# A duo's transposes in the beat of its products, and three attentions of the first block as one chain

## The chip, the cores and the metric

The kernel runs on one core of one Trainium2 chip, in one launch. The metric is device time in microseconds (us) of that core; lower is better. PE is TensorE, DVE is VectorE, ACT is ScalarE, POOL is GpSimd and SP is SyncE, which issues the loads of the weights.

## The reference

One transformer block with three attentions, followed by two layers of a second block, all on `x` of 512 tokens by 1024 channels in fp32. Cut to what matters here:

```python
# first block: three attentions on one normed h, then a gated merge, then an MLP
oa = diff_attention(aq, ak, av, lam, bias_a)                  # "att_a": 4 heads, two softmax maps each, w = p0 - lam*p1
oa = rms_norm(oa, diff_subln) * (1.0 - lam_init)
ob = banded_attention(bq, bk, bv, bias_b, B_WINDOW, sinks)    # "att_b": 8 heads, window of 128, a sink in the softmax
oc = g0 * o_cmp + g1 * o_sel + g2 * o_win                     # "att_c": compressed, selected and window branch
x = x + sum_n(sigmoid(mg_n) * (branch_n @ w_branch_n)) @ w_out
x = x + square(relu(rms_norm(x) @ w_up)) @ w_down
# second block, twice: SwiGLU, mixer, SwiGLU
ya = chunked_relpos_attention(qa, ka, va, ...)                # "att_a2"
yc = forgetting_attention(qc, kc, vc, ...)                    # "att_c2"
# each attention: s = q k^T * scale + bias; p = softmax(mask(s)); o = p v
# (queries and keys are rms-normed per head: a "root" each in the kernel)
```

## The kernel before

Everything is held transposed, channels in the 128 partitions and tokens along the free axis. A dense product of the weights is a *group*: 8 chunks of 128 input channels, each chunk three matmuls (L1202 to L1204: high by high, high by low and low by high parts of an fp32 split), 128x512 or, for tokens in partitions, 128 tokens by 408 or 512. POOL splits each weight piece into its two parts. PSUM has 8 banks; a group takes one of its ring.

An attention is cut into *duos*: two heads (or two maps) of one block of 128 queries. There are 16 in att_a, att_b, att_a2 and att_c2, and 48 in att_c, where each block has three branches. A duo goes through these steps:

- `score` (PE, L1275): two products of queries and keys, into banks 0 and 1; then `minima` on DVE (L1704) adds the bias, writes the duo's tile of `s_sb` (two duos fit) and leaves `row_min`.
- `exp` (ACT, L1445, twice), then the inverses of the sums (DVE, L1717, in att_c L1721 and L1730, in a column of the sum bank 4).
- `prob` (ACT, L1463; in att_a L1455, L1457 and then DVE L1734, which joins the two maps): the scaled probabilities.
- `turn` (PE, L1292): one transpose of 128x128 for each block of keys, into bank 2 (att_a, att_b) or banks 2 and 3. It waits for `probs`.
- `copy` (ACT, L1478): the transposes to `pt_sb`, of which there is one. It waits for the turn and for the products of the duo before.
- `pv` (PE, L1312 in att_a, L1317 elsewhere): the products with the values, into bank 5. Behind the last duo of a pair the result leaves the bank, and in att_a it goes through a root of its own ("differential": ACT L1405 and L1407, PE L1261, ACT L1415, DVE L1663 and L1673, ACT L1545, DVE L1676).

The banks of the scores come free for the next duo when att_a's `probs` are there (the second map lies in bank 1 until then), elsewhere when `row_min` is.

The order on every engine is written out by a planner that runs in Python before the build: `plan` puts steps into one list, `ORDER`, and every engine walks this list and emits its part of each step. Nothing is reordered later. `attend` gives the duos of one attention as *beats*, each a function with a weight; `weave` runs a beat and then as many *stretches* (two chunks of a group, so six matmuls) as the beat's share of the weight asks for. Beat j holds the scores of duo j + 2, the turn of duo j + 1 and the products of duo j. Within the beat of att_a, of att_b and att_c and att_c2, and of att_a2 the order of these differs (the three branches at the end of `attend`).

A root of queries or keys is spread over the stretches by `LATER`: its sum on PE two stretches after the group, the two halves of its reciprocal (DVE L1663) three and four after. `ROOTED` is the last root whose steps stand in `ORDER`. `HELD` says for each bank what its next user must wait for. Each `weave` ends with `flush`, which puts out all of `LATER`.

The load of the bias of the pair after next (`load_bias`) stands right behind the last scores of a pair. ACT issues it, after a wait for that duo's `row_min` (L1491).

## Time and profile before

| | us |
|---|---|
| median of 3 runs (lowest, highest) | 3510.7 (3504.93, 3511.44) |
| the profiled execution's own time | 3509.4 |
| its span | 3507.6 |
| PE busy | 3407.7 (97%) |
| POOL busy | 2370.5 (68%) |
| DVE busy | 1186.1 (34%) |
| ACT busy | 883.3 (25%) |

By the times of their scores (L1275) the stages lie at: att_a 98 to 233, att_b 233 to 332, att_c 332 to 545, att_a2 1460 to 1590 and 2706 to 2836, att_c2 behind each of these. What lies between is dense products.

The profile is of one execution. An engine's row in a timeline has its start, its duration, and in brackets how long the engine was idle before it and which instruction released it. A wait can be small in the sum and still decide, since PE is busy nearly all the time: what PE is idle is what could be gained, with what its clock loses behind a wait.

### The profile page before, as it was taken

Reading aid. Unit: us, or ns where it says so; the run is one execution under the profiler, and the core shown is the slowest. Engines: PE = TensorE matmul, PEld = TensorE weight load, DVE = VectorE, ACT = ScalarE, POOL = GpSimd, SP = SyncE. Lnnn points to the kernel's source line nnn. Section 1 sums busy time; section 2 is a strip of 40 time slices with the busy share of each in tenths; the row PEclk is TensorE's granted clock in tenths of the full one; section 3 lists DMA queues with packets and bytes.
Section 4 is the critical chain, followed back from the end, with each engine's and each line's share of the span. In section 5 each row is a group of like instructions: output and inputs, shape, how many; then the busy total and the mean of one; then the engine's idle time right before and its main releaser. Section 6 shows DMA issues by size and latency. Waiting matters only on the chain.

```text
span 3507.6 us, 42466 instructions
## 1 busy us (share of the span) xinstructions
PE 3407.7 (97%) x17034; PEld 2738.9 (78%) x17034; DVE 1186.1 (34%) x2514; ACT 883.3 (25%) x1876; POOL 2370.5 (68%) x1242
## 2 busy tenths in 40 slices
PE   8978999999999999999999999999999999999999
PEld 6655777988898888667779888888887677798887
DVE  6554342433443234552223111332245422241111
ACT  2656552211120002354312000210012543221000
POOL 7514547787778776645677877687775546678775
PEclk9999999999999999999999999999999999999999
DMA  3212223344535442212232222254432222223232
GB/s 142 68 60 82 73 64 102 143 175 168 187 132 198 175 165 94 73 58 82 85 103 102 96 97 95 80 218 167 170 129 73 67 75 79 82 97 103 98 100 73
DMA packets 104771, 388.08 MB, mean 111 GB/s; under 512 B 12016, under 2 KB 12400, under 8 KB 98432
## 3 DMA queue, kind: packets, MB, share of 16 engines
q1 hardware_dynamic: 88272, 292.76, 25.3%
q10 hardware_dynamic: 16304, 92.62, 6.9%
q8 instruction: 135, 2.21, 0.3%
q14 instruction: 60, 0.49, 0.0%
HBM read 383.20 MB, written 2.13 MB: 110 GB/s over the span
## 4 chain that ended last, share of the span: by engine, by line
PE 91%; DVE 4%; ACT 4%; issue 1%; ACTq 0%; DVEq 0%
PE psum L1202 28%; PE psum L1204 27%; PE psum L1203 27%; PE psum L1275 2%; PE psum L1317 2%; PE psum L1292 2%; PE psum L1261 1%; DVE rs_t L1663 1%; DVE s_sb L1704 1%; ACT s_sb L1445 0%; ACT s_sb L1463 0%; ACT L1445 0%; ACT L1415 0%; PE psum L1253 0%; ACT rs_t L1415 0%
## 5 line engine op out<-in xcount | busy, mean ns | idle before, releaser
L1170 POOL TENSOR_TENSOR w_hi<-raw,ones 128x1024 fp32r<-128x1024 f32 (+2 forms) x593 | 1041.3, 1756 | 981.0 <-PE psum L1204 973.1
L1173 POOL TENSOR_TENSOR w_lo<-raw,w_hi 128x1024 fp32r<-128x1024 f32 (+2 forms) x593 | 1316.4, 2220 | 46.5
L1202 PE MATMUL psum<-h_hi,w_hi 128*128 128x512 f32 (+2 forms) x2912 | 1141.9, 392 | 30.5 <-DVE r L1679 20.5
L1204 PE MATMUL psum<-h_hi,w_lo 128*128 128x512 f32 (+2 forms) x2912 | 1106.2, 380 | 0.0
L1203 PE MATMUL psum<-h_lo,w_hi 128*128 128x512 f32 (+2 forms) x2912 | 1105.6, 380 | 0.0
L1202 PEld LDWEIGHTS psum<-h_hi,w_hi 128*128 128x128 f32 (+1 forms) x2912 | 550.3, 189 | 167.4 <-issue 33.9
L1204 PEld LDWEIGHTS psum<-h_hi,w_lo 128*128 128x128 f32 (+1 forms) x2912 | 550.1, 189 | 106.7
L1203 PEld LDWEIGHTS psum<-h_lo,w_hi 128*128 128x128 f32 (+1 forms) x2912 | 551.0, 189 | 101.0 <-issue 7.2
L1202 PE MATMUL psum<-a_hi,w_hi 128*128 128x512 f32 (+1 forms) x1064 | 392.5, 369 | 0.0
L1203 PE MATMUL psum<-a_lo,w_hi 128*128 128x512 f32 (+1 forms) x1064 | 391.9, 368 | 0.0
L1204 PE MATMUL psum<-a_hi,w_lo 128*128 128x512 f32 (+1 forms) x1064 | 391.8, 368 | 0.0
L1930 DVE TENSOR_TENSOR psum<-g_sb,psum 128x512 f32<-128x512 f32 x120 | 83.5, 696 | 734.3 <-PE psum L1204 641.4
L1595 ACT ACTIVATE g_sb<-psum 128x512 f32<-128x512 f32 x120 | 71.8, 598 | 919.5 <-PE psum L1204 832.9
L1204 PEld LDWEIGHTS psum<-a_hi,w_lo 128*128 128x128 f32 x1064 | 200.6, 188 | 33.5
L1203 PEld LDWEIGHTS psum<-a_lo,w_hi 128*128 128x128 f32 x1064 | 200.6, 189 | 33.4
L1202 PEld LDWEIGHTS psum<-a_hi,w_hi 128*128 128x128 f32 x1064 | 200.6, 189 | 33.3
L1939 DVE SCALAR_TENSOR_TENSOR x<-psum,res,x 128x512 f32<-128x512 f32 (+1 forms) x132 | 88.4, 669 | 357.5 <-PE psum L1204 357.5
L1602 ACT ACTIVATE a_hi<-psum 128x512 fp32r<-128x512 f32 x120 | 71.8, 598 | 493.9 <-DVE psum L1930 493.9
L1704 DVE CUSTOM_DVE_ANT_0 s_sb<-psum,bias_t 128x128 f32<-128x128 f32 (+3 forms) x224 | 100.8, 487 | 233.1 <-PE psum L1275 159.9
L1445 ACT ACTIVATE s_sb<-s_sb,row_min 128x128 f32<-128x128 f32 (+6 forms) x272 | 140.1, 517 | 130.5 <-DVE row_min L1704 127.3
L1795 DVE CUSTOM_DVE_ANT_0 ada_t<-ada_t,psum 128x1024 f32<-128x1024 f32 x144 | 167.7, 1215 | 0.0
L1663 DVE RECIPROCAL rs_t<-rs_t 128x256 f32<-128x256 f32 x78 | 132.3, 1729 | 68.2 <-ACT rs_t L1415 68.2
(198 smaller groups left out, 3305.0 us busy)
## 6 DMA issues: line engine op xcount, KB each, us to landing
raw<-weights_dram SPq DMA_DIRECT2D x487, 512.0 KB, 3.4
ada_t<-ada_dram ACTq DMA_DIRECT2D x48, 1536.0 KB, 7.1
raw<-weights_dram SPq DMA_DIRECT2D x76, 256.0 KB, 2.7
raw<-weights_dram SPq DMA_DIRECT2D x32, 384.0 KB, 3.1
bias_t<-biases_dram ACTq DMA_DIRECT2D x36, 256.0 KB, 2.9
bias_t<-cum_dram ACTq DMA_DIRECT2D x16, 256.0 KB, 4.1
out_dram<-x SPq DMA_DIRECT2D x8, 256.0 KB, 2.0
raw<-weights_dram SPq DMA_DIRECT2D x4, 408.0 KB, 3.2
```

Source lines behind the costliest of these rows:

```text
L1170: nc.gpsimd.tensor_tensor(high, piece, ones[:, 0:1].to_broadcast([P, n]), ALU.mult)\
L1173: nc.gpsimd.tensor_tensor(w_lo[:, p % NR, 0:n], piece, high.bitcast(F32), ALU.subtract)\
L1202: mm(dst, lh, rh, start=first, stop=False)
L1203: mm(dst, lh, rl, start=False, stop=False)
L1204: return mm(dst, ll, rh, start=False, stop=last)
L1445: ins = fn(to, s, ACT.Exp, scale=-1.0, bias=row_min[:, r:r + 1], accum_out=row_sum[:, r:r + 1])
L1595: fn(g_sb[:, g.index % 2, :], bank(g.bank), ACT.Silu if gated else ACT.Relu)\
L1663: v.reciprocal(r, r).then_inc(sem["qk_inverse"], 1)
L1704: ins = v.tensor_tensor_reduce(out=s[:, 0:w], in0=bank(SCORE_BANKS[half], w), in1=tile, scale=-1.0, scalar=sinks[:, half:half + 1] if o el ...
L1795: ins = v.tensor_tensor_reduce(out=part, in0=part, in1=c_bcast, scale=1.0, scalar=0.0, op0=ALU.mult, op1=ALU.add, accum_out=mod_raw[:, l, ...
L1930: v.tensor_tensor(bank(g.bank), g_sb[:, n % 2, :], bank(g.bank), ALU.mult)\
L1939: v.scalar_tensor_tensor(x[:, d, cs], bank(g.bank)[:, cs], res_of(which, d), x[:, d, cs], ALU.mult, ALU.add).then_inc(sem["x_added"], 1)
```

## The change

- In all attentions the turn and the copy of a duo move from the beat before its products into the beat of its products: beat j now holds the scores of duo j + 2, the turn of duo j, its copy and its products.
- All attentions have one order: turn, scores, copy; exps; products; low part and `prob`. The branches for att_a and for att_a2 are gone.
- A `Chain` holds the duos of one or of several attentions. The first block's three are one chain: the last two beats of att_a hold the first two scores of att_b, and those of att_b the first two of att_c. `flush` stands only behind the chain's last attention.
- Where a step needs a root whose steps still stand in `LATER`, the planner pulls them forward: before scores whose queries or keys are not rooted, before a turn whose bank a root still holds, and before scores of the compressed branch.
- The wait for the sum bank in att_c is taken at `prob` and not at the scores, and `HELD` names the inverses as its last user.

```diff
--- before.py
+++ after.py
@@ -190,9 +190,10 @@
         pass
 
 
-def weave(kind, layer, jobs):
-
-    beats = attend(kind, layer)
+def weave(chain, kind, jobs):
+
+
+    beats = attend(chain, kind)
     total, weight = sum(job.n for job in jobs if isinstance(job, Group)), sum(w for _, w in beats)
     q, done, passed_by = stretches(jobs), 0, 0
     for beat, w in beats:
@@ -202,7 +203,8 @@
             done += next(q, total)
     for _ in q:
         pass
-    flush()
+    if chain.duos[-1].kind == kind:
+        flush()
 
 
 
@@ -504,16 +506,29 @@
     return (Q_AT[u.kind], 4 + u.pair)
 
 
-def attend(kind, layer):
-
-
-    duos = duos_of(kind, layer)
+@dataclass(eq=False)
+class Chain:
+
+    duos: list
+    masks: list
+
+
+def chain_of(kinds, layer):
+    return Chain([u for kind in kinds for u in duos_of(kind, layer)], [])
+
+
+def attend(chain, kind):
+
+
+    duos, masks = chain.duos, chain.masks
     n = len(duos)
-    masks = []
+    own = [j for j in range(n) if duos[j].kind == kind]
+    lo, hi = (own[0] if own[0] else -2), own[-1] + 1
 
     def scores(j):
         if j + 2 < n:
             u = duos[j + 2]
+            kind = u.kind
             u.n = tick("scores")
             for name in ("probs", "transposed", "pt_copied", "pv"):
                 assert tick(name) == u.n
@@ -522,17 +537,19 @@
             u.s_before = [take(b) for b in SCORE_BANKS]
             HELD[SCORE_BANKS[0]] = HELD[SCORE_BANKS[1]] = ("probs", u.n) if kind == "att_a" else ("row_min", 2 * u.n)
             u.need = max(READY[(Q_AT[kind], u.pair)], READY[keys_of(u)])
-            if kind == "att_c":
-                u.inv_before = take(SUM_BANK)
+            while u.need > ROOTED[0] or u.br == "cmp" and "kc_done" not in TOTAL:
+                LATER.pop(0)[1]()
             put("score", u)
             if u.last:
                 load_bias(u.bias.n + 2, 2 * u.n)
                 masks.append([2, u.bias.n + 2])
 
     def turns(j):
-        if 0 <= j + 1 < n:
-            u = duos[j + 1]
-            u.t_before = [take(b) for b in (T_BANKS[:1] if kind in ("att_a", "att_b") else T_BANKS)]
+        if 0 <= j < n:
+            u = duos[j]
+            u.t_before = [take(b) for b in (T_BANKS[:1] if u.kind in ("att_a", "att_b") else T_BANKS)]
+            while any(at and at[0] == "qk_out" and at[1] > ROOTED[0] for at in u.t_before):
+                LATER.pop(0)[1]()
             for b in T_BANKS[:len(u.t_before)]:
                 HELD[b] = ("pt_copied", u.n)
             put("turn", u)
@@ -540,6 +557,7 @@
     def products(j):
         if 0 <= j:
             u = duos[j]
+            kind = u.kind
             if u.first:
                 u.o_before = take(O_BANK)
             u.need_v = READY[V_AT[kind]]
@@ -561,34 +579,32 @@
                 mask_bias(e[1])
 
     def copy(j):
-        if 0 <= j + 1 < n:
-            put("copy", duos[j + 1])
+        if 0 <= j < n:
+            put("copy", duos[j])
 
     def exps(j):
         if j + 2 < n:
             put("exp", duos[j + 2])
 
     def low(j):
-        if 0 <= j and duos[j].last and kind != "att_a":
+        if 0 <= j and duos[j].last and duos[j].kind != "att_a":
             put("blow", duos[j])
 
     def scale(j):
         if j + 2 < n:
-            put("prob", duos[j + 2])
+            u = duos[j + 2]
+            if u.kind == "att_c":
+                u.inv_before = take(SUM_BANK)
+                HELD[SUM_BANK] = ("inverses", 2 * u.n)
+            put("prob", u)
 
     out = []
-    for j in range(-2, n):
+    for j in range(lo, hi):
         w = 1 + max([d.blocks for d in duos[max(0, j):j + 3]])
-        if kind == "att_a":
-            out += [(lambda j=j: scores(j), w), (lambda j=j: (exps(j), turns(j)), w),
-                    (lambda j=j: (products(j), copy(j), scale(j)), 2 * w)]
-        elif kind in ("att_b", "att_c", "att_c2"):
-            out += [(lambda j=j: (scores(j), products(j)), w), (lambda j=j: (exps(j), low(j)), w),
-                    (lambda j=j: (turns(j), copy(j)), w), (lambda j=j: scale(j), w)]
-        else:
-            out += [(lambda j=j: scores(j), w), (lambda j=j: (exps(j), turns(j)), w),
-                    (lambda j=j: (products(j), copy(j)), w), (lambda j=j: (low(j), scale(j)), w)]
-    return out + [(lambda: [mask_bias(b) for _, b in masks], 0)]
+
+        out += [(lambda j=j: (turns(j), scores(j), copy(j)), w), (lambda j=j: exps(j), w),
+                (lambda j=j: products(j), w), (lambda j=j: (low(j), scale(j)), w)]
+    return out + [(lambda: [mask_bias(b) for _, b in masks], 0)] * (hi == n)
 
 
 
@@ -864,9 +880,9 @@
             chain += shifts + [product]
     jobs += chain
     put("tables")
-    weave("att_a2", l, jobs)
+    weave(chain_of(("att_a2",), l), "att_a2", jobs)
     ring = MIX_RINGS["att_c2"]
-    weave("att_c2", l, merge((l + 1, 1), "br_b", "set", ring) + merge((l + 1, 0), "br_a", "mid", ring))
+    weave(chain_of(("att_c2",), l), "att_c2", merge((l + 1, 1), "br_b", "set", ring) + merge((l + 1, 0), "br_a", "mid", ring))
     if l == 0:
         tick("cond_loaded", 16)
         put("condload")
@@ -919,15 +935,16 @@
           normed(("ck", 4), "key", ("small", "gain", 7), ("k5", 2), ring),
           plain(("ck", 0), ("k5", 3), ring), plain(("ck", 1), ("k5", 4), ring)]
     tick("gate_tanh")
-    weave("att_a", 0, [ks[0]] + b + ks[1:] + token_groups(("vbc",), V_BC, "v_bc", ring)
+    chain = chain_of(("att_a", "att_b", "att_c"), 0)
+    weave(chain, "att_a", [ks[0]] + b + ks[1:] + token_groups(("vbc",), V_BC, "v_bc", ring)
           + [lambda: put("gates", TOTAL["plain_out"])])
 
     ring = MIX_RINGS["att_b"]
     cq = [normed(("cq", i), "query", ("small", "gain", 4), ("r2", i), ring) for i in range(4)]
     gather, hidden = compress(ring)
-    weave("att_b", 0, [lambda: gather(0), cq[0], lambda: gather(1), cq[1], hidden, cq[2], cq[3]])
+    weave(chain, "att_b", [lambda: gather(0), cq[0], lambda: gather(1), cq[1], hidden, cq[2], cq[3]])
     ring = MIX_RINGS["att_c"]
-    weave("att_c", 0, merge((0, 0), "br_a", "set", ring) + merge((0, 1), "br_b", "mid", ring))
+    weave(chain, "att_c", merge((0, 0), "br_a", "set", ring) + merge((0, 1), "br_b", "mid", ring))
     tick("cond_loaded", 16)
     put("condload")
     run_all(merge((0, 2), "br_c", "last"))
```

What this moves, at three places. In the functions of the engines the lines of the kernel after are 17 higher.

ScalarE in att_a, where the root of the second pair's result ends: `br_a` is that root's high part (it waits for `qk_out`, a result of DVE), the two rows with `row_sum` are a duo's exps, `pt_sb<-psum` is a copy. Before:

```order
L1491 DMA bias_t<-biases_dram 128x512 [waits row_min]
L1491 DMA bias_t<-biases_dram 128x512
L1545 ACTIVATE br_a<-psum 128x512 [waits qk_out]
L1445 ACT_TABLE_LOAD
L1445 ACTIVATE s_sb,row_sum<-s_sb,row_min 128x384
L1445 ACTIVATE psum,row_sum<-s_sb,row_min 128x384
L1478 ACTIVATE pt_sb<-psum 128x256 [waits pv,transposed]
L1455 ACTIVATE s_sb<-s_sb,row_inv 128x384 [waits inverses]
```

After:

```order
L1495 ACTIVATE pt_sb<-psum 128x512 [waits pv,transposed]
L1462 ACT_TABLE_LOAD
L1462 ACTIVATE s_sb,row_sum<-s_sb,row_min 128x384
L1462 ACTIVATE psum,row_sum<-s_sb,row_min 128x384
L1562 ACTIVATE br_a<-psum 128x512 [waits qk_out]
L1472 ACTIVATE s_sb<-s_sb,row_inv 128x384 [waits inverses]
L1474 ACTIVATE row_scale<-row_inv,neg_lam 128x1 [waits inverses]
```

The exps now stand ahead of `br_a`, and the copy stands ahead of the exps and no longer between them and `prob` (`s_sb<-s_sb,row_inv`); the bias's DMAs stand ahead of the copy.

ScalarE some duos later, at the last bias load of att_a. Before:

```order
L1545 ACTIVATE br_a<-psum 128x512 [waits qk_out]
L1491 DMA bias_t<-biases_dram 128x512 [waits row_min]
L1491 DMA bias_t<-biases_dram 128x512
L1445 ACTIVATE s_sb,row_sum<-s_sb,row_min 128x128
L1445 ACTIVATE psum,row_sum<-s_sb,row_min 128x128
L1478 ACTIVATE pt_sb<-psum 128x512 [waits pv,transposed]
```

After:

```order
L1562 ACTIVATE br_a<-psum 128x512 [waits qk_out]
L1508 DMA bias_t<-biases_dram 128x512 [waits row_min]
L1508 DMA bias_t<-biases_dram 128x512
L1495 ACTIVATE pt_sb<-psum 128x256 [waits pv,transposed]
L1462 ACTIVATE s_sb,row_sum<-s_sb,row_min 128x128
L1462 ACTIVATE psum,row_sum<-s_sb,row_min 128x128
```

The copy of the duo two before (128x256), which stood well ahead of these rows, now stands behind the two DMAs, and so behind the wait for `row_min`.

TensorE where att_b ends and att_c begins: `h_hi`, `w_hi` rows are dense products, `pt_sb,v_bc` the products with the values, `sq_t,cst` the sum of the last query root, `k_56,r_52` scores of att_c, `cst,s_sb` transposes. Before:

```order
L1203 MATMUL psum<-h_lo,w_hi 128x512
L1204 MATMUL psum<-h_hi,w_lo 128x512
L1317 MATMUL psum<-pt_sb,v_bc 64x128 [waits pt_copied]
L1317 MATMUL psum<-pt_sb,v_bc 64x128
L1261 MATMUL psum<-sq_t,cst 128x512 [waits qk_rooted,qk_squared]
L1275 MATMUL psum<-k_56,r_52 128x128 [waits row_min]
L1275 MATMUL psum<-k_56,r_52 128x128
L1202 MATMUL psum<-h_hi,w_hi 128x512 [waits w_lo,qk_out]
L1203 MATMUL psum<-h_lo,w_hi 128x512
```

After:

```order
L1220 MATMUL psum<-h_lo,w_hi 128x512
L1221 MATMUL psum<-h_hi,w_lo 128x512
L1334 MATMUL psum<-pt_sb,v_bc 64x128 [waits pt_copied]
L1334 MATMUL psum<-pt_sb,v_bc 64x128
L1278 MATMUL psum<-sq_t,cst 128x512 [waits inverses,qk_squared]
L1309 MATMUL psum<-cst,s_sb 128x128 [waits qk_out,probs]
L1309 MATMUL psum<-cst,s_sb 128x128
L1292 MATMUL psum<-kc_sb,r_52 128x31 [waits kc_done,row_min]
L1292 MATMUL psum<-kc_sb,r_52 128x31
L1219 MATMUL psum<-h_hi,w_hi 128x512 [waits w_lo]
```

Before, scores and two stretches of dense products stood behind the root's sum. Now a turn stands right behind it, and waits for that root (`qk_out`), since its second bank was the root's.

## Rows read from the trace of the kernel before

**Rows 1.** The page's busy times over the whole span, by engine.
```profile
...
PE 3407.7 (97%) x17034; PEld 2738.9 (78%) x17034; DVE 1186.1 (34%) x2514; ACT 883.3 (25%) x1876; POOL 2370.5 (68%) x1242
```

**Rows 2.** Windows, by stage: length, busy by engine, granted clock, DMA share, GB/s.
```profile
...
98.00:233.00 135.00, 114.19 (x522) 83.80 (x520) 69.68 (x146) 82.53 (x170) 54.09 (x35) 0.94 0.21 67
233.00:332.00 99.00, 74.87 (x450) 48.09 (x448) 57.56 (x169) 66.57 (x158) 33.49 (x28) 0.91 0.25 80
332.00:545.00 213.00, 212.33 (x1294) 151.43 (x1294) 77.01 (x389) 118.33 (x334) 102.90 (x67) 0.99 0.21 64
1460.00:1590.00 130.00, 122.12 (x615) 81.54 (x614) 59.14 (x152) 69.96 (x151) 62.79 (x32) 0.97 0.19 63
```

**Rows 3.** Waits of PE in att_a: us in total, times, longest.
```profile
...
PE psum L1275 <- DVE s_sb L1734: 15.0, 10, 5.6
PE psum L1261 <- DVE br_a L1676: 3.7, 1, 3.7
```

**Rows 4.** Waits of PE in att_b and at its two ends.
```profile
...
PE psum L1275 <- DVE row_min L1704: 9.2, 3, 5.9
PE psum L1317 <- ACT pt_sb L1478: 8.9, 6, 1.9
PE psum L1362 <- ACT cmp_g L1566: 3.0, 1, 3.0
```

**Rows 5.** Timeline around att_a's longest wait: start, us, engine, instruction, [idle before].
```profile
...
191.35 0.60 ACT L1545 ACTIVATE br_a<-psum 128x512 fp32r<-128x512 f32 x1 [5.18 <-DVE psum L1673]
...
191.98 0.69 DVE L1676 TENSOR_TENSOR br_a<-psum,br_a 128x512 fp32r<-128x512 f32 x1 [0.66 <-ACT br_a L1545]
...
193.26 0.61 ACT L1445 ACTIVATE s_sb<-s_sb,row_min 128x384 f32<-128x384 f32 x1
...
196.23 1.65 PE L1275 MATMUL psum<-r 64*128 64x384 f32 x4 [5.57 <-DVE s_sb L1734]
```

**Rows 6.** Timeline in att_a: a copy behind the products, and the next scores.
```profile
...
203.06 0.49 ACT L1478 ACTIVATE pt_sb<-psum 128x384 f32<-128x384 f32 x1 [3.09 <-PE psum L1312]
...
204.95 0.70 PE L1275 MATMUL psum<-r 64*128 64x256 f32 x4 [0.87 <-DVE s_sb L1734]
```

**Rows 7.** Timeline where att_a ends and att_b begins.
```profile
...
235.07 3.36 DVE L1663 RECIPROCAL rs_t<-rs_t 128x256 f32<-128x256 f32 x2 [1.86 <-ACT rs_t L1415]
...
241.38 1.22 PE L1275 MATMUL psum<-k,r 64*128 64x256 f32 x4 [5.88 <-DVE row_min L1704]
```

**Rows 8.** Timeline where att_b ends and att_c begins.
```profile
...
320.52 1.12 PE L1261 MATMUL psum<-sq_t,cst 128*128 128x512 f32 x2 [0.32 <-ACT sq_t L1405]
...
323.00 3.36 DVE L1663 RECIPROCAL rs_t<-rs_t 128x256 f32<-128x256 f32 x2 [1.31 <-ACT rs_t L1415]
...
327.62 0.49 PE L1275 MATMUL psum<-k,r 64*128 64x128 f32 x4 [2.60 <-DVE row_min L1704]
```

**Rows 9.** Timeline, bias loads: the wait for one, the issues of another.
```profile
...
118.50 1.28 ACT L1415 ACT_TABLE_LOAD   x1 [2.66 <-DVE row_min L1704]
...
188.89 0.82 ACTq L1491 DMA_DIRECT2D bias_t<-biases_dram  x2
```

**Rows 10.** Groups by form (copies), and of the page (reciprocals of the roots).
```profile
...
L1478 ACT ACTIVATE pt_sb<-psum 128x512 f32<-128x512 f32 x40 | 23.5, 588 | 29.0 <-PE psum L1292 24.1 <-PE psum L1312 3.6 <-PE psum L1317 1.1
...
L1663 DVE RECIPROCAL rs_t<-rs_t 128x256 f32<-128x256 f32 x78 | 132.3, 1729 | 68.2 <-ACT rs_t L1415 68.2
```

**Rows 11.** Timeline of PE: the products that follow a group of transposes.
```profile
...
111.32 0.48 PE L1202 MATMUL psum<-h_hi,w_hi 128*128 128x512 f32 x1
111.64 0.40 PE L1203 MATMUL psum<-h_lo,w_hi 128*128 128x512 f32 x1
111.87 0.40 PE L1204 MATMUL psum<-h_hi,w_lo 128*128 128x512 f32 x1
```

**Rows 12.** Windows right behind the two longest waits.
```profile
...
194.00:200.00 6.00, 3.77 (x10) 2.54 (x11) 2.16 (x8) 3.31 (x10) 3.26 (x5) 0.59 0.01 5
242.00:248.00 6.00, 4.92 (x15) 3.10 (x12) 4.96 (x17) 2.27 (x9) 0.00 (x0) 0.50 0.00 0
```

## The prediction

> **What bounds the kernel now.** I read the page first. PE is busy 3407.7 of 3507.6 us [rows 1], so all that any reordering can win is PE's idle 100 us, and what its clock loses. The change moves no work on or off PE. So the next view is the windows by stage [rows 2]: att_a has 135.00 - 114.19 = 20.8 us of idle PE and a mean granted clock of 0.94, att_b 24.1 us and 0.91, att_c 0.7 us, att_a2 7.9 us. A clock of 0.94 means that (1 - 0.94) x 2 x 135 = 16 us lay at the lower of the two levels, 0.91 in att_b another 18 us; half of such time is lost where PE has work, at its busy share of 80% some 14 us in all. The stages that the change touches hold 45 us of waits and 14 us of clock in att_a and att_b, and little elsewhere. Then the waits of these two stages: in att_a PE waits for att_a's joined maps before it may overwrite their banks, 15.0 us in ten waits, and once 3.7 us for the sum bank [rows 3]; in att_b it waits for `row_min` 9.2 us, for copies 8.9 us and for the compressed branch's gelu 3.0 us [rows 4]. Last the timeline at the longest of them, for what stands ahead of what on ACT and DVE.
>
> **att_a, joined maps: 6 us less.** A duo's scores need the probabilities of the duo before, so scores, minima, exps, inverses, `prob` and the joining are a loop. In the longest wait (5.57 us) the exps stood behind the root's `br_a` on ACT, which started at 191.35, and a table load, and began at 193.26 [rows 5]. In the new order they stand ahead of it. What is late next is DVE: its inverses come behind L1676, which ends at 191.98 + 0.69 = 192.67. From the first exp to the scores it took 196.23 - 193.26 = 2.97 us, less two exps of 0.6 some 1.75 us: scores at 194.4 in place of 196.2, so 1.8 us less. A copy no longer stands between exps and `prob`; in [rows 6] it waited for the products until 203.06 and the scores then waited 0.87 us: such a wait goes. The other nine waits sum to 15.0 - 5.6 = 9.4 us; where a reciprocal of a root is what is late (half of them) the copy's move does nothing. I take 9.4 to 5. The 3.7 us for the sum bank falls to about 2.3, because the joining and two inverses now stand behind the root's last steps and not between them. The remaining 2.1 us (20.8 - 15.0 - 3.7) go with the early turn. Against that stand: `prob` now comes one sub-beat later, so in five duos a half reciprocal and the scaling of a root (1.73 + 0.75 us, the latter an estimate by rows of 128x512 like L1676's 0.69) slip between exps and inverses. Part of it lies beside the exps; I take 2 us. And the bias loads, below, 1.5 us. Sum: -1.8 - 4.4 - 1.4 - 2.1 + 2 + 1.5 = -6. Bounds: all 20.8 gone, or 16 us of root work fully exposed, +12.
>
> **From att_a to att_b: 5.5 us less.** Before, the last result's root ran with nothing behind it: its reciprocals took 3.36 us of DVE from 235.07, the first minima of att_b came behind them, and PE waited 5.88 us [rows 7]. Now two scores of att_b stand ahead of that root and its sum stands between att_b's first groups. What is late next is the gather of the compressed branch and the same reciprocals on DVE, ahead of `row_min` of the fourth duo; by their lengths I leave 1.5 us, and a turn's wait of 1 us behind it goes too: -5.5. Bounds -7 and 0.
>
> **att_b's middle: 0.** From turn to products lies one stretch in 13 of 16 duos and none in three; before it was one in 12 and none in four. So no cover is lost. ACT has half a beat more before a copy is due, which would take perhaps 4 of the 8.9 us [rows 4]. The bias loads take it back: a load waits for the minima of the duo just scored, and the copy is now queued behind it. ACT sat idle 2.66 us for this once, and two issues take 0.82 us [rows 9]; with a copy of 0.59 us [rows 10] that is about 2.5 us behind the scores, against one stretch of six products at 0.23 us [rows 11], 1.4 us. So 1.1 us at each of four pairs: +4.4. Bounds -8 and +10.
>
> **From att_b to att_c: 3.5 us more.** The last query root ends in bank 3, which the first turn of att_c needs. Before, scores and two stretches stood behind that root's sum at 320.52, and the wait was 2.60 us at 327.62 and about 1 more behind it, 4 with the small one ahead [rows 8]. Now the turn stands right behind the sum, and queued behind that turn is all of PE. The sum itself waits for the inverses of the second duo. From the end of the group: a square, two exps, the high part and `prob`, 2.8 us of ACT, a table load of 1.28, the square root 0.7, reciprocals 3.36 [rows 8], the scaling 0.75: 8.9 us, of which PE works 1.5. That is 7.4 for 4. Bounds 0 and +7.
>
> **att_c, att_a2, att_c2: 4 us more.** In att_c ten duos have no stretch between turn and products (before two), mostly short ones whose copy the scores cover; of four bias loads two have none and two have one: 2 x 2 + 2 x 1.1 minus what their waits hid, 4 us; bounds 0 and +12. In att_a2 two stretches (before five) stay between turn and products, 2.7 us for a copy and the rest of ACT's queue; a few waits for `prob` go, a few for copies come: 0, bounds -5 and +8. att_c2 keeps its three: 0.
>
> **Fewer switches on PE: 3.4 us less.** Between dense products and small ones PE changes 34 times less (43 to 33 groups in att_a, 48 to 36 in each att_a2, four more in att_b and att_c; counted in the order). The first product behind a group of transposes starts its successor 0.32 us later, the next ones 0.23 [rows 11]: 0.1 us each. By the Trainium skill, TensorE: Matmul & The Clock Gate, in "Part 2: What happens when you issue a matmul", the loads of weights are pulled ahead of products in flight, which would make such a switch free, and the sum 3.4 us less good. The row has 0.1 us, so the trace does not agree.
>
> **Clock: 5 us less.** The longest waits are followed by windows with a granted clock of 0.59 and 0.50 [rows 12]. One of the two (att_b's start) should go and one stay, and the new wait at att_c keeps its own. Of 14 us I take 5 back. Bounds +5 and -14.
>
> **Sum.** -6 - 5.5 + 0 + 3.5 + 4 - 3.4 - 5 = -12.4. The profiled execution took 3509.4 us, 1.8 more than its span, so 3497.0. The median of the runs is 1.3 above that execution: 3498.
>
> **Rivals.** (1) *It loosens nearly all.* With prompt copies the loop in att_a falls under its beat, att_b runs without waits but for gelu, and the clock stays up: 30 of 45 us, 9 of clock and the switches: 3468. For it: the mean beat in att_a is 7.5 us, a loop without roots some 5. Against it: roots, table loads and reciprocals stay where they are. (2) *Given back.* The waits for joined maps turn into waits for copies, which now have 1 or 2 stretches of cover instead of 3 or 4 in att_a: gains and losses meet within 0.2%, about 3508. For it: ACT is busy 82.53 of 135 us there, and a copy stands behind whatever ACT has late. (3) *Slower: `prob` behind the root in att_a.* The bank is held until the maps are joined. If the 16 us of reciprocals, scalings and square roots that now stand between exps and `prob` in five duos lie fully open, the clock falls behind each, and I get 3509.4 + 12 - 5.5 + 3.5 + 4 - 3.4 + 5 = 3525. It decides when PE's waits for the joined maps pass 25 us. Against it: the same reciprocals stood ahead of the next minima in the same loop before. (4) *It doesn't do what it says:* a forced root stands somewhere else too. The order shows it at att_c's start alone.
>
> **How the numbers follow.** My case 0.45, (1) 0.15, (2) 0.22, (3) 0.14, (4) 0.04. About 0.2% (7 us) is what a measurement here tells from no change, so faster means under 3503.7. My case is faster for three quarters of its width, and with (1) and some of (2) that gives 0.56 faster, 0.26 within, 0.18 slower. The range of 8 in 10 goes from 3474 to 3518.
>
> **What would show it.** Right: PE's waits for att_a's maps at 8 to 11 us, the wait at att_b's start under 3 us, att_b's window some 5 us shorter, a wait of 6 to 8 us for a query root at the first transposes of att_c, copies waited for behind bias loads, a clock of 0.96 in att_a. Wrong: longer waits for the maps, copies waited for by PE in att_a or att_a2 for more than 8 us, or att_c longer by more than 6.

## The result, and the profile after

The changed kernel takes 3547.8 us (median of 4 runs, 3546.7 to 3549.0) against 3511.1 for the kernel before (4 runs). The ratio is 1.0109, 95% interval 1.0093 to 1.0125: slower by 37 us. The forecast was 3498, 12 us faster. The profiled execution has a span of 3545.0 us, 37.4 longer than before.

The page's busy times answer to [rows 1]:

```profile
...
PE 3423.5 (97%) x17034; PEld 2745.5 (77%) x17034; DVE 1192.2 (34%) x2514; ACT 887.7 (25%) x1876; POOL 2369.9 (67%) x1242
```

PE is busy 15.8 us more for the same 17034 instructions, and idle 121.5 us, 21.6 more. By stage, windows of the changed kernel (length, busy by engine, granted clock, DMA share, GB/s), which answer to [rows 2]:

```profile
...
96.00:221.00 125.00, 104.05 (x479) 75.73 (x477) 69.24 (x145) 80.06 (x162) 52.76 (x35) 0.96 0.17 58
221.00:327.00 106.00, 77.45 (x474) 50.67 (x473) 59.95 (x169) 68.44 (x163) 33.80 (x29) 0.93 0.27 90
327.00:562.00 235.00, 227.54 (x1308) 157.14 (x1306) 76.23 (x389) 121.65 (x335) 103.23 (x67) 0.98 0.18 59
1480.00:1617.00 137.00, 124.94 (x614) 84.49 (x613) 61.94 (x152) 70.83 (x153) 63.01 (x32) 0.95 0.18 60
```

The windows are cut at the scores, and the chain moves these against the dense products: att_a's 125 us hold 479 matmuls for 522 in 135 us, att_b's 106 hold 474 for 450 in 99, att_c's 235 hold 1308 for 1294 in 213; only att_a2's 137 and 130 hold the same, 614 and 615. Their lengths can't be compared as they are. To see where the time goes, I lay the starts of the same duo's scores side by side in two traces. Duos are counted through the program: 1 to 16 are att_a, 17 to 32 att_b, 33 to 80 att_c, 81 to 96 the first att_a2, 97 to 112 att_c2, and so on. The columns give what a stretch is longer than in the kernel before, in us; the variants are told below.

| from duo to duo | changed | x1 | x2 | x4 | x5 | x9 |
|---|---|---|---|---|---|---|
| start to 1 | -2.5 | -2.7 | -2.3 | -2.4 | -2.1 | +0.2 |
| 1 to 16, att_a | -5.1 | -4.2 | -5.4 | -6.8 | -9.7 | -5.0 |
| 16 to 19, border | -12.7 | -1.7 | -12.5 | -15.5 | -15.5 | -15.5 |
| 19 to 33, att_b | +9.2 | +12.3 | +17.7 | +2.1 | +2.5 | +10.7 |
| 33 to 37, border | +9.2 | -1.6 | -1.1 | +7.6 | +9.9 | -0.2 |
| 37 to 80, att_c | +18.8 | +14.8 | +0.1 | +14.6 | +11.1 | -0.1 |
| 81 to 96, att_a2 | +6.8 | +6.7 | +5.6 | +5.4 | +3.3 | -1.4 |
| 113 to 128, att_a2 | +7.7 | +7.7 | +7.8 | +5.5 | +5.8 | -0.5 |
| span | +37.4 | +36.9 | +13.1 | +15.9 | +8.3 | -10.4 |

The first 2.5 us lie ahead of every moved instruction and come and go between kernels whose order is equal there; they are not the change's. PE's idle time up to duo 1 is 17.4 or 17.5 us in every trace; what differs is its own time.

These marks don't part equal work either: with a chain the scores of a duo stand ahead of dense products that stood ahead of them before. So here is, for the same stretches, how many dense products start in them (one is 0.23 us where nothing waits), and how long PE is idle in them:

| from duo to duo | dense: before, changed | idle: before, changed | idle: x1 | x2 | x4 | x9 | x10 | x12 |
|---|---|---|---|---|---|---|---|---|
| 1 to 16, att_a | 270, 264 | 18.6, 18.3 | 18.1 | 18.0 | 15.5 | 15.7 | 18.6 | 15.4 |
| 16 to 19, border | 60, 48 | 9.1, 2.6 | 6.7 | 2.6 | 0.0 | 0.0 | 6.7 | 0.0 |
| 19 to 33, att_b | 78, 84 | 13.5, 20.0 | 17.3 | 21.8 | 14.4 | 14.7 | 10.7 | 14.3 |
| 33 to 37, border | 36, 36 | 3.6, 8.6 | 2.9 | 3.6 | 8.5 | 3.5 | 3.9 | 3.6 |
| 37 to 80, att_c | 528, 540 | 0.1, 6.3 | 5.3 | 0.1 | 3.6 | 0.0 | 0.0 | 0.0 |

x1 and x10 have the kernel before's dense products in every row, x4 those of the changed one; x2, x9 and x12 have those of the changed kernel up to duo 19, then 96 to duo 33, and those of before from there. The lines of the windows that the first rows and the last rest on, before (two) and changed (three):

```profile
...
98.64:219.33 120.69, 102.06 (x452) 73.11 (x451) 65.52 (x136) 77.75 (x155) 51.62 (x31) 0.93 0.18 56
219.33:249.71 30.38, 21.25 (x95) 16.25 (x95) 15.46 (x39) 12.31 (x31) 1.83 (x4) 0.83 0.27 87
```

```profile
...
96.17:211.80 115.63, 97.31 (x447) 69.96 (x446) 65.09 (x136) 77.80 (x154) 51.15 (x31) 0.97 0.17 58
211.80:229.47 17.67, 15.03 (x82) 13.36 (x82) 6.59 (x23) 6.06 (x22) 1.82 (x4) 0.90 0.32 107
338.77:560.45 221.68, 215.36 (x1260) 149.44 (x1259) 72.94 (x369) 115.49 (x320) 101.62 (x67) 0.99 0.19 61
```

By its marks the changed kernel is 18 us ahead at duo 19, but 18 dense products (4.2 us) lie behind the mark that lay ahead of it. PE's waits up to there fell by 6.8 us. From duo 19 to 37 they grow by 11.4, in att_c by 6.3. At duo 81, where both have done the same work, the changed kernel is 20.3 us behind, 12.7 of it idle time and 7.6 PE's own; each att_a2 then adds 7 or 8.

A trace is one execution, and one program's own time on PE scatters: x9 and x12 are the same up to duo 81, and PE is idle for 58.9 and 58.3 us up to there, yet stands 7 us apart. So idle time is the firmer measure of a stage, and differences of a few us in the first table, up to duo 37, are not.

The waits of PE in att_a, which answer to [rows 3]: the maps (L1292) are waited for as long as before, and copies are new (L1329).

```profile
...
PE psum L1292 <- DVE s_sb L1751: 14.7, 10, 3.7
PE psum L1329 <- ACT pt_sb L1495: 4.2, 2, 2.6
PE psum L1278 <- DVE br_a L1693: 2.0, 1, 2.0
```

In att_b and at its ends, for [rows 4]: copies 19.6 us in place of 8.9, and the forced root's 5.1 with 2.7 for its sum.

```profile
...
PE psum L1334 <- ACT pt_sb L1495: 19.6, 14, 2.8
PE psum L1309 <- DVE r L1696: 5.1, 1, 5.1
PE psum L1278 <- DVE row_scale L1747: 2.7, 1, 2.7
PE psum L1379 <- ACT cmp_g L1583: 0.6, 1, 0.6
```

In att_c copies are waited for 8.9 us where nothing was:

```profile
...
PE psum L1334 <- ACT pt_sb L1495: 7.0, 6, 1.9
PE psum L1321 <- ACT pt_sb L1495: 1.9, 3, 0.9
```

### The profile page after: what moved, and what is told of

Read it like the earlier page. It is cut to its first block, busy times and chain, and to the rows that moved or that the text cites. A ratio compares the mean times of both kernels' runs of the same rounds, so it can differ in the third digit from the quotient of the medians.

```text
span 3545.0 us, 42490 instructions
## 1 busy us (share of the span) xinstructions
PE 3423.5 (97%) x17034; PEld 2745.5 (77%) x17034; DVE 1192.2 (34%) x2514; ACT 887.7 (25%) x1876; POOL 2369.9 (67%) x1242
## 4 chain that ended last, share of the span: by engine, by line
PE 90%; DVE 5%; ACT 4%; issue 1%; ACTq 0%; DVEq 0%
PE psum L1219 28%; PE psum L1220 27%; PE psum L1221 27%; PE psum L1292 2%; PE psum L1334 2%; PE psum L1309 2%; PE psum L1278 1%; DVE rs_t L1680 1%; DVE s_sb L1721 1%; ACT s_sb L1462 1%; ACT pt_sb L1495 0%; ACT s_sb L1480 0%; ACTq L1508 0%; ACT L1462 0%; DVE r L1696 0%
## 5 line engine op out<-in xcount | busy, mean ns | idle before, releaser
L1187 POOL TENSOR_TENSOR w_hi<-raw,ones 128x1024 fp32r<-128x1024 f32 (+2 forms) x593 | 1041.0, 1755 | 1029.6 <-PE psum L1221 1021.0
L1190 POOL TENSOR_TENSOR w_lo<-raw,w_hi 128x1024 fp32r<-128x1024 f32 (+2 forms) x593 | 1316.1, 2219 | 46.6
L1221 PEld LDWEIGHTS psum<-a_hi,w_lo 128*128 128x128 f32 x1064 | 200.5, 188 | 33.3
```

Of the source, the lines that this page charges most:

```text
L1187: nc.gpsimd.tensor_tensor(high, piece, ones[:, 0:1].to_broadcast([P, n]), ALU.mult)\
L1190: nc.gpsimd.tensor_tensor(w_lo[:, p % NR, 0:n], piece, high.bitcast(F32), ALU.subtract)\
L1221: return mm(dst, ll, rh, start=False, stop=last)
```

## The experiments

The theory after the first comparison: 18 us won by the chain and att_a's order, lost again because copies come late and because transposes next to scores cost PE more than products next to scores; in att_a2 a collision of VectorE and GpSimd. Rivals: the forced root and the chain are the cost, or the late copies alone. All runs were timed in five rounds beside the kernel before (3509.6 to 3511.1 us in these). x1 to x4 ran together, then x5 to x8, then x9 to x12.

**x1: three chains.** The new order, each attention a chain of its own.

```diff
-    chain = chain_of(("att_a", "att_b", "att_c"), 0)
+    chain = chain_of(('att_a',), 0)
...
+    chain = chain_of(('att_b',), 0)
...
+    chain = chain_of(('att_c',), 0)
```

> The changed kernel with the new order of each attention kept, but the first block's three attentions as three chains again: each runs out before the next begins, and the next begins with a prologue of its own. Theory (the chain is about neutral: it wins 5 to 12 us where att_b starts and pays 8 us where att_c's first transposes drag the first query's root forward; the loss of 37 us comes from the order inside the duos): 3545 to 3555 us, with the windows of att_b and att_c as long as in the changed kernel but for the two borders. Rival (the chain with its forced root is the main cost): 3520 to 3530 us. If it wins back nothing at b to c and loses the 12 us at a to b: 3560 us.

Measured: 3546.9 us (3546.4 to 3551.6), ratio 1.0108 [1.0095, 1.0121]. The chain is neutral, within 1 us. By PE's idle time it wins 4.1 us at the first border (2.6 for 6.7) and pays 2.7 in att_b, 5.7 at the second border and 1.1 in att_c; the larger steps between the marks of the two hold moved products. The rival is dead: the loss stands in the duos' order.

**x2: att_c and att_c2 as before.** New order in att_a, att_b and att_a2, one chain over the first two.

```diff
+        elif kind in ("att_b", "att_c", "att_c2"):
+            out += [(lambda j=j: (scores(j), products(j)), w), (lambda j=j: (exps(j), low(j)), w),
+                    (lambda j=j: (turns(j + 1), copy(j + 1)), w), (lambda j=j: scale(j), w)]
```

> The new order in att_a, att_b and both att_a2, with one chain over att_a and att_b; att_c is a chain of its own in the order of before, and both att_c2 are in the order of before. Theory (a turn that stands next to its scores costs PE 0.2 us a duo more in att_c than products next to scores did, and the copies wait behind exponentials there; the border b to c costs 8 us; the two att_c2 cost 1 us): att_c wins back 19 us, the border with its end 11, so 3516 to 3521 us; what stays of the loss is att_b's 9 to 14 us and twice 7 us in att_a2, less 18 won up to att_b's start. Rival (copies in att_b alone, the rest follows from when they end): 3535 to 3545 us.

Measured: 3522.1 us (3519.5 to 3522.5), ratio 1.0033 [1.0021, 1.0045]. att_c's 18.8 us are gone to 0.1. att_b's +17.7 for +9.2 is mostly work: it holds 96 dense products for 84, and some 15 small ones more. By idle time, att_b and the second border together cost 25.4 us for 28.6, so taking the chain off before att_c wins 3.2 us; with the late loads of x4 it wins 5 (17.9 in x12 for 22.9 in x4).

**x3: att_a alone.** The order of the kernel before, with the new one in att_a and nowhere else (built from the changed kernel, by putting the old branches and three chains back).

> The kernel before with one edit: att_a alone in the new order; no chain, all other attentions as before. Theory: att_a is the one stage in which the new order shortens the waits (for the copies of its maps); it wins 5 to 9 us up to att_a's end, so 3502 to 3506 us. Rival (what was won up to att_b's start came from the chain alone): 3511 us, no change. Rival (the gain in att_a is given back where att_b starts): 3509 to 3513 us with a longer wait at att_b's first duos.

Measured: 3509.7 us (3509.0 to 3514.8), ratio 1.0000 [0.9992, 1.0009]. No change: from duo 1 to 17 it is 1.6 us shorter, and PE's idle time from duo 1 to 16 is 18.3 us for 18.6. The first rival holds: att_a's new order shortens no wait, and the waits that fell ahead of att_b fell at the border. Without a chain PE is idle there for 7.8 us (9.1 before), so the last rival, a longer wait, is out.

**x4: bias loads behind the exponentials.** One move in the changed kernel.

```diff
             put("score", u)
-            if u.last:
-                load_bias(u.bias.n + 2, 2 * u.n)
-                masks.append([2, u.bias.n + 2])
...
     def exps(j):
         if j + 2 < n:
             put("exp", duos[j + 2])
+            u = duos[j + 2]
+            if u.last:
+                load_bias(u.bias.n + 2, 2 * u.n)
+                masks.append([2, u.bias.n + 2])
```

> The changed kernel with one move: ScalarE issues the load of the next bias behind the duo's exponentials, not between its scores and the copy of the maps of the duo two back, so that the copy no longer waits for the row minima that release the bias (4 loads in each attention). Theory (copies come late mainly behind these loads in att_b and att_c): 3536 to 3542 us, with the waits of products for copied maps down from 34 us to about 22. Rival (the copies are late because of the exponentials and reciprocals in front of them): 3546 to 3549 us. Rival (the loads now come late for their masks): 3555 us with new waits for the bias before row minima.

Measured: 3525.3 us (3522.0 to 3526.9), ratio 1.0042 [1.0030, 1.0054]: 22 us back, twice what the theory gave. The timeline of the changed kernel at one of the loads (start, duration, engine, instruction, idle before): DVE's second minimum ends at 238.75, the two issues of the load take 0.82 us, and only then the copy runs that PE waits for.

```profile
...
238.67 0.08 DVE L1721 DVE_READ_ACCUMULATOR2_ANT row_min<- 128x1 f32 x1
...
238.78 0.82 ACTq L1508 DMA_DIRECT2D bias_t<-biases_dram  x2
239.70 0.60 ACT L1495 ACTIVATE pt_sb<-psum 128x512 f32<-128x512 f32 x1 [1.07 <-DVE row_min L1721]
...
240.35 0.66 PE L1334 MATMUL psum<-pt_sb,v_bc 128*64 128x128 f32 x8 [2.51 <-ACT pt_sb L1495]
```

The same place in x4, where the copy starts before that minimum is done:

```profile
...
234.15 0.57 ACT L1496 ACTIVATE pt_sb<-psum 128x512 f32<-128x512 f32 x1
234.28 0.08 DVE L1722 DVE_READ_ACCUMULATOR2_ANT row_min<- 128x1 f32 x1
...
234.77 0.66 PE L1335 MATMUL psum<-pt_sb,v_bc 128*64 128x128 f32 x8 [1.32 <-ACT pt_sb L1496]
...
236.04 0.82 ACTq L1509 DMA_DIRECT2D bias_t<-biases_dram  x2
```

The wait is 1.32 us for 2.51. The order differs by that move alone, so at this place the load ahead of the copy costs 1.2 us. The waits for copies fall from 4.2 to 0 in att_a, from 18.7 to 11.6 between duos 19 and 33, by 2.8 between 37 and 80. In all PE is idle 17.8 us less and busy 3.7 less (3419.8), the latter at a clock of 0.98 for 0.96 in att_b. x5, x6 and x8 have x4's order up to duo 33, and show how far one trace can be trusted: att_b stands at +2.1, +2.5, +5.9 and +4.3 us, PE's idle time in it at 14.4, 13.7, 15.4 and 14.0 for 20.0 in the changed kernel.

**x5: scores next to products in att_c and att_c2**, on x4.

```diff
+        if kind in ("att_c", "att_c2"):
+            out += [(lambda j=j: (turns(j), copy(j)), w), (lambda j=j: (scores(j), products(j)), w),
+                    (lambda j=j: (exps(j), low(j)), w), (lambda j=j: scale(j), w)]
+            continue
```

> The changed kernel with the bias loads behind the exponentials (3525 us by its own run), and in att_c and both att_c2 a duo's transposes alone with the copy right behind them, then dense products, then the next scores next to the products of the same duo, as they stood before: the chain stays. Theory (PE works 10 us longer in att_c because scores and value products no longer stand together: 0.23 us a duo for 44 duos, and copies add 5 us of waiting): att_c shrinks by 10 to 15 us from first to last duo, each att_c2 by 0.7 us, so 3509 to 3514 us. Rival (only the waits for copies cost, the neighbours are equal): 3519 to 3522 us, and PE's busy time in att_c stays near 235 us. Rival (the switch is the same but the copies have less cover here): 3526 us or more.

Measured: 3519.4 us (3517.5 to 3521.4), ratio 1.0031 [1.0019, 1.0042], 6 us below x4 where the theory had 11 to 16. PE's work in att_c falls as the theory said (205.7 us for 213.8 in x4, with 6 dense products less), but its waits rise as the second rival said (8.3 us for 3.6). The time is the first rival's, which had PE's work unchanged: that it is not. The windows from duo 37 to duo 80, of the kernel before, x1 and x5:

```profile
...
340.62:543.45 202.83, 202.77 (x1247) 145.35 (x1246) 74.38 (x373) 113.25 (x318) 97.22 (x64) 1.00 0.21 65
```

```profile
...
342.74:560.34 217.60, 212.34 (x1247) 147.38 (x1246) 73.77 (x373) 115.93 (x319) 97.30 (x65) 0.99 0.20 60
```

```profile
...
325.81:539.75 213.94, 205.65 (x1254) 148.40 (x1253) 73.51 (x369) 114.86 (x318) 100.08 (x67) 1.00 0.20 63
```

x1 has the same 1247 matmuls as before and PE is busy 9.6 us longer with them, at the same clock within 0.01, and waits for copies 5.2 us: together the 14.8. x5 has 205.7 us for 1254 (6 of the 7 more are dense, 1.4 us), so the neighbours account for most of the 9.6; but its copy has one beat of dense products to run beside where the order before had two (the turn stood ahead of `scale`), and the waits are 7.7 us.

Where the 9.6 us come from is read in the starts. Before, around a duo without waits:

```profile
...
425.76 0.39 PE L1204 MATMUL psum<-h_hi,w_lo 128*128 128x512 f32 x1
426.08 0.49 PE L1275 MATMUL psum<-k,r 64*128 64x128 f32 x4
426.50 1.09 PE L1317 MATMUL psum<-pt_sb,v_bc 128*64 128x128 f32 x16
427.52 0.50 PE L1202 MATMUL psum<-h_hi,w_hi 128*128 128x512 f32 x1
...
429.02 0.38 PE L1290 MATMUL psum<-cst,s_sb 128*31 128x128 f32 x2
429.15 0.48 PE L1202 MATMUL psum<-h_hi,w_hi 128*128 128x512 f32 x1
```

and in x1:

```profile
...
449.69 0.39 PE L1223 MATMUL psum<-h_hi,w_lo 128*128 128x512 f32 x1
449.92 0.38 PE L1309 MATMUL psum<-cst,s_sb 128*31 128x128 f32 x2
450.23 0.49 PE L1294 MATMUL psum<-k,r 64*128 64x128 f32 x4
450.76 0.43 PE L1323 MATMUL psum<-pt_sb,vc_sb 31*64 31x128 f32 x4
451.12 0.50 PE L1221 MATMUL psum<-h_hi,w_hi 128*128 128x512 f32 x1
```

From the start of two transposes to the dense product behind them it is 0.13 us (429.02 to 429.15), but to scores behind them 0.31 (449.92 to 450.23). Over all duos from 37 to 80, the median time from the last start of one kind to the first of the next is, in us:

| | before | x1 |
|---|---|---|
| dense to score / turn to score | 0.326 | 0.202 |
| score to products | 0.306 | - |
| score to dense | - | 0.306 |
| dense to products | - | 0.319 |
| products to dense | 0.202 | 0.202 |
| dense to turn | 0.232 | 0.232 |
| turn to dense | 0.028 | - |
| sum | 1.094 | 1.261 |

So a duo costs 0.167 us more, 7.2 us for 43; 1.9 more lie between dense products (113.3 us for 111.4, x452 each). Of these 1.1 belong to the neighbours too: the first dense product behind transposes is followed by the next after 0.314 us, behind scores or value products after 0.337, elsewhere after 0.231.

**x6: the pool's operations made one**, on x4.

```diff
-                v.tensor_scalar(src[:, 16:S], src[:, 16:S], 1.0 / 2 ** (g + 1), None, ALU.mult)
...
-                v.tensor_tensor(pool_d[:, n % 2, :], src, region["r1"][:, g, :], ALU.subtract)
+                v.tensor_tensor(pool_d[:, n % 2, 0:16], src[:, 0:16], region["r1"][:, g, 0:16], ALU.subtract)
...
+                v.scalar_tensor_tensor(pool_d[:, n % 2, 16:S], src[:, 16:S], 1.0 / 2 ** (g + 1),
+                                       region["r1"][:, g, 16:S], ALU.mult, ALU.subtract)
```

> The changed kernel with the bias loads behind the exponentials (3525 us), and in the pooling of both att_a2 VectorE's last two full-width operations (scale by a constant, then subtract; 0.42 and 0.69 us where nothing is beside them) made one operation on 496 columns and one on 16. Theory (in each att_a2 these two are held up by GpSimd's weight splits that run at the same time, 2.0 and 2.7 us, and the pool's product on PE waits 4 us for them and then runs at the low clock): with one of the two gone the wait falls to about 2 us and each att_a2 shrinks by 2 to 4 us, so 3517 to 3521 us. Rival (the fused operation is held up as long as both were): 3525 us, wait still 4 us. Rival (the 6 us come from the new order of the duos and not from the pool's product): 3525 us with the wait gone.

Measured: 3519.8 us (3515.7 to 3521.3), ratio 1.0028 [1.0017, 1.0038]. PE's wait falls from 4.5 us in x4 to 2.2, and att_a2 from +5.4 to -0.6 and from +5.5 to +0.5. These are 11 us where the medians differ by 5.5: up to duo 81, where the two programs are the same, x6's profiled execution is 4.6 us behind x4's. The timeline of the changed kernel there:

```profile
...
1537.83 1.89 POOL L1187 TENSOR_TENSOR w_hi<-raw,ones 128x1024 fp32r<-128x1024 f32 x1 [4.07 <-PE psum L1221]
...
1538.00 2.00 DVE L1849 TENSOR_SCALAR pool_s<-pool_s 128x496 f32<-128x496 f32 x1
...
1539.80 2.39 POOL L1190 TENSOR_TENSOR w_lo<-raw,w_hi 128x1024 fp32r<-128x1024 f32 x1
1540.03 2.71 DVE L1854 TENSOR_TENSOR pool_d<-pool_s,r 128x512 f32<-128x512 f32 x1
...
1542.80 2.08 PE L1392 MATMUL psum<-pool_d,lay 128*128 128x512 f32 x2 [4.03 <-DVE pool_d L1854]
```

DVE's scale and subtraction (L1849, L1854) end 0.3 and 0.55 us behind POOL's two splits (L1187, L1190), after 2.00 and 2.71 us. Before, POOL began later and they ran free, in 0.42 and 0.69:

```profile
...
1519.04 0.42 DVE L1832 TENSOR_SCALAR pool_s<-pool_s 128x496 f32<-128x496 f32 x1
...
1519.49 0.69 DVE L1837 TENSOR_TENSOR pool_d<-pool_s,r 128x512 f32<-128x512 f32 x1
...
1520.11 1.89 POOL L1170 TENSOR_TENSOR w_hi<-raw,ones 128x1024 fp32r<-128x1024 f32 x1 [5.33 <-PE psum L1204]
```

x6 shows it from both sides: 16 columns take 1.75 us on DVE until POOL's first is done (1524.68 + 1.90), then the wide one runs in 0.68, and POOL's second, begun at the same time, takes 2.89 for the 2.39 above.

```profile
...
1524.68 1.90 POOL L1188 TENSOR_TENSOR w_hi<-raw,ones 128x1024 fp32r<-128x1024 f32 x1 [4.07 <-PE psum L1222]
1524.85 1.75 DVE L1852 TENSOR_TENSOR pool_d<-pool_s,r 128x16 f32<-128x16 f32 x1
1526.64 0.68 DVE L1855 SCALAR_TENSOR_TENSOR pool_d<-pool_s,r 128x496 f32<-128x496 f32 x1
1526.66 2.89 POOL L1191 TENSOR_TENSOR w_lo<-raw,w_hi 128x1024 fp32r<-128x1024 f32 x1
```

The Trainium skill, SBUF — State Buffer, section "SBUF: two separate sides", says that VectorE and GpSimd share a pair of ports as an exclusive lock, for the whole instruction, where VectorE has two inputs in SBUF or runs in a faster mode of two ports. As far as POOL's spans go, which are rough, the rows agree: whichever begins first runs in its own time and the other waits for its end. What the new order changes is the moment: a split that began 0.6 us behind the subtraction's start now begins ahead of both.

**x7: the kernel before with x4's move.**

> The kernel before with one edit, ScalarE issues the next bias load behind the exponentials and not ahead of them. Theory (in the order before the copy is not behind this load, since it stands in another beat; only exponentials are, which wait for the row minima themselves): 3506 to 3511 us. Rival (the load ahead of the exponentials costs as much there as in the changed kernel, so the 22 us have nothing to do with the change): 3490 to 3500 us.

Measured: 3502.8 us (3501.0 to 3505.7), ratio 0.9983 [0.9974, 0.9991]: 6.7 us won, between the theory and its rival, against 22 in the changed kernel. The load costs something in either order, and some three times as much where the copy stands behind it.

**x8: a mix**: x5 with both att_a2 in the order of before.

> Bias loads behind the exponentials; att_a and att_b in the new order, att_c and both att_c2 with scores next to products and the transposes alone, one chain over the first block's three attentions; both att_a2 in the order of before. Theory (each part's price is its own, and the stages add): 3525 less 15 in att_c, 1.4 in att_c2 and 2 times 6 in att_a2, so 3494 to 3500 us, 10 to 15 us faster than the kernel before. Rival (the gains up to att_b are made by PE's idle being moved and come back in att_c): 3507 to 3512 us.

Measured: 3512.2 us (3508.8 to 3515.6), ratio 1.0010 [1.0001, 1.0018]. att_a2 came as expected (-1.3 and -0.3), att_c did not: with its border it is 19.6 us longer than before, where the theory left 7. One sub-beat of cover is too little there (8.3 us of idle time in att_c), and a chain into att_c is idle for 8.4 to 8.6 us at the border (33 to 37) in all five runs that have it, for 3.6 before. The rival's time came, not for its reason.

**x9 to x12: what pays.** x9: new order in att_a and att_b with a chain over them, everything else in the order of before, x4's and x6's edits. x10: the same with three chains. x11: the kernel before with the two edits. x12: x9 with both att_a2 in the new order.

> New order in att_a and att_b with one chain over the two; att_c (a chain of its own), both att_c2 and both att_a2 in the order of before; the bias loads behind the exponentials everywhere; the pool's last two full-width VectorE operations made one. Theory (stages add: 15 us ahead of before when att_c is reached, as in the run with late bias loads; nothing lost in att_c; 1 us won in each att_a2): 3491 to 3497 us, ratio 0.995 to 0.997. Rival (what is won up to att_b's end is owed at the border to att_c, whose queries' roots end late either way): 3501 to 3505 us, like the kernel before with late bias loads alone.

> As the run above, but with three chains in the first block, so att_b starts with a prologue of its own. Theory (the chain is neutral in the changed kernel because att_b there gives back what the border won; with the late bias loads att_b gives back only 2 us, so the chain is worth 5 to 10 us now): 3499 to 3504 us. Rival (the chain moves waits and is worth nothing here either): within 2 us of the run above.

> The kernel before with the bias loads behind the exponentials and the two pool operations made one; its order of duos untouched. Theory (the pool's operations are met by GpSimd's splits only in the new order of att_a2): 3500 to 3504 us, the time of late bias loads alone (3503). Rival (they cost here as well, in waits that other work hides badly): 3495 to 3499 us.

> As the first of these runs, but both att_a2 in the new order. Theory (with the pool's operations made one, the order of att_a2 makes no difference: -0.6 and +0.5 us were measured for it against before): within 2 us of the first of these runs, 3491 to 3499 us. Rival (the new order in att_a2 has a price of its own beside the pool's operations): 3 us or more above it.

| | us, median (lowest to highest) | ratio [95%] |
|---|---|---|
| x9 | 3493.2 (3490.7 to 3499.0) | 0.9948 [0.9935, 0.9960] |
| x10 | 3501.7 (3499.2 to 3502.2) | 0.9970 [0.9958, 0.9981] |
| x11 | 3502.6 (3499.8 to 3504.9) | 0.9974 [0.9964, 0.9985] |
| x12 | 3497.6 (3496.7 to 3498.6) | 0.9959 [0.9946, 0.9973] |

x9 beats both kernels: 18 us under before, 55 under the changed one. The profile is of x9's longest execution, so the first table shows less. The chain from att_a to att_b is worth 8.4 us by the medians (x10 less x9), and by PE's idle time from duo 1 to 37 some 6 (39.8 us in x10, 34.0 in x9, 33.3 in x12); x7 and x11 are equal, so the pool's edit does nothing in the old order. x12 lies 4.3 us above x9. The runs of the two overlap, but the stages agree: each att_a2 is 2.5 and 2.7 us longer than in x9, 1.4 of it idle time, since a wait of 2.2 us for the pool (as in x6) stays. The theory is wrong there, and its rival right.

## Why the prediction was wrong

Its own steps, beside what the stretches of the table measured:

- **att_a, -6**: -5.1 to duo 16 with the chain. The size is near by luck, the reasons are not: PE is idle 18.3 us for 18.6. What is shorter is its own time, 97.3 us for 102.1: 1.4 is six dense products that moved, and the rest goes with a clock of 0.97 for 0.93, which the same order shows as 94.2 us in one trace (x5) and 99.8 in another (x8). The waits for maps stayed at 14.7 us [rows 3] where I had 8 to 11; alone the order of att_a is worth nothing (x3). The longest is 3.7 for 5.57, but the other nine sum to 11.0 for 9.4.
- **att_a to att_b, -5.5**: -12.7 between the marks, but 2.8 of that are 12 dense products that moved, two small ones went with them, and the clock is 0.90 for 0.83. PE's waits there fell by 6.5 us (2.6 for 9.1), inside my bound of 7. This step held, mechanism and size (without the chain, in x1, they fell by 2.4).
- **att_b's middle, 0**: the first step that failed, +9.2 here and +12.3 in x1. I had +4.4 for the bias loads and set against it 4 us that ACT's half beat would win. The half beat won nothing: turn to products is what counts, and in that stretch ACT now has a load's wait, its issues, and often a table load. Moving the loads took PE's idle time in att_b from 20.0 us to 13.7 to 15.4 (x4, x5, x6, x8), so they cost 4.6 to 6.3 us there for my 4.4: I had the queue right and priced a load at 1.1 us of waiting, where the one shown above made PE wait 2.51. And I set the loads at 1.5 us in att_a and 4 with short duos in att_c; over the whole kernel they cost 22 (x4).
- **att_b to att_c, +3.5**: +9.2, of which PE's idle time is 4.9 (8.6 for 3.6); 16 small products more lie between these marks. The waits came as worked out (5.1 and 2.7 us, 7.8 for my 7.4). But PE's clock fell behind them:

```profile
...
319.61 2.04 PE L1278 MATMUL psum<-sq_t,cst 128*128 128x512 f32 x2 [2.65 <-DVE row_scale L1747]
326.71 0.66 PE L1309 MATMUL psum<-cst,s_sb 128*128 128x128 f32 x2 [5.05 <-DVE r L1696]
...
328.45 0.63 PE L1220 MATMUL psum<-h_lo,w_hi 128*128 128x512 f32 x1
...
333.18 0.40 PE L1220 MATMUL psum<-h_lo,w_hi 128*128 128x512 f32 x1
```

  The sum takes 2.04 us for the 1.12 of [rows 8], and dense products 0.63 until 332.8, 0.40 from there. The root stood forced. Without it PE waits for roots elsewhere, but less: 3.2 us less in x2, 5 with the late loads.
- **att_c, att_a2, att_c2, +4**: the largest miss. +18.8 in att_c alone (2.8 of it 12 dense products that moved in), 6.8 and 7.7 in att_a2, 0.65 in each att_c2. In att_c the copies' waits (5.2 us in x1, 6.3 in the changed kernel) were what I priced at 4; the 9.6 us of PE's own work were in no term but the next, with the other sign. In att_a2 the collision of DVE and POOL was in no term either.
- **Switches, -3.4**: the step whose sign was wrong. I counted changes between dense and small products and gave each the 0.1 us of [rows 11]. That is what the second dense product behind transposes is late by (0.314 us for 0.231), and not the whole price. What counts is which two kinds meet. Behind transposes a dense product starts at once (0.028 us), behind scores after 0.306; products behind scores cost 0.306, behind dense ones 0.319. The old order let the dense products follow the cheap neighbour. By the Trainium skill, TensorE: Matmul & The Clock Gate, "Part 2: What happens when you issue a matmul", the next product's weights load while this one runs, which by itself leaves nothing to pay for a change. The 0.028 us agrees; 0.306 to 0.326 between unlike tiles, for 0.231 between dense products, do not.
- **Clock, -5**: 0.96 for 0.94 in att_a, 0.93 for 0.91 in att_b, but 0.98 for 0.99 in att_c and 0.95 for 0.97 in att_a2: what one stage gained the next gave back.

Up to duo 81 the forecast, without the terms of the att_a2 stages, had the changed kernel 10 to 12 us ahead; it stood 20 behind, 12.7 of them waits and 7.6 PE's own time, and both att_a2 added 14.5.

Of the rivals, (3) was slower for another reason: the waits for maps stayed under its 25 us. (2) named the true mechanism, waits for copies, but its "gains and losses meet" was a guess about a size. My test "copies waited for more than 8 us in att_a or att_a2" did not fire (4.2 and 0.7); "att_c longer by more than 6" did.

Open: 1.5 of the 3.3 us between att_c's last duo and att_a2's first (1.8 are waits, 9.3 us for 7.5), and how much of PE's own time, with x4's 3.7 us of it, is the clock behind waits and how much is scatter.

## What to carry to other kernels

When a step is moved between queues, look at what stands between it and its consumer on every engine: here the bias loads, four in each attention, two DMA issues behind a wait in ScalarE's queue, cost 22 us until they were put behind the exponentials. Ask of a reordering which kinds of matmul become neighbours, not how many groups there are. And move order stage by stage: the same edit won 6.5 us of waits at one border and lost 6.4 in the stage behind it, and in att_c it cost 6.3 of waits and some 10 of TensorE's own time. When two traces are laid side by side at a step that the edit moves, count the work ahead of the mark in both: here 20 matmuls passed for a gain of time.

## What the hardware showed

- On PE, by starts: from the last transpose of 128x128 to a dense product 0.028 us (and 0.314 from that to the next, for 0.231 in a run of them), to a product on 64 rows 0.202; from one on 64 rows to a dense one 0.306; from a dense one to one on 64 rows or columns 0.32. In att_c2, whose scores end in a full 128x128 product, the dense one follows after 0.028 again, and the new order costs 0.65 us for 16 duos there, where 0.167 each would be 2.7.
- A VectorE operation of 16 columns took 1.75 us while GpSimd ran a 1024-column operation, and GpSimd's next took 0.5 us more while VectorE ran.
